# Eight neighbouring rows per partition for the experts' gate and up weights, and every eighth feature as the gather's stationary tile

## The reference

```python
def expert(y, p):
    wg, wu, wd, ge = p
    a = jax.nn.silu(t @ wg) * (t @ wu) * ge[:, None].astype(t.dtype)
    return y + a @ wd, None
```

## Time and profile before

| | |
|---|---|
| Median of 3 runs | 1677.74 us (1676.63 to 1678.19) |
| Profiled execution, own time | 1684.68 us |
| Its span | 1682.9 us |
| Mean granted TensorE clock | 0.922 |
| TensorE busy with matmuls / weight loads | 1461.1 us (87%) / 790.2 us (47%) |
| VectorE, ScalarE, GpSimd busy | 430.0, 258.2, 70.5 us |
| Moved by DMA | 345.99 MB, 206 GB/s over the span |
| Expert stage of layer 0 (gate and up of the first expert to the last down) | 410.9 to 693.5 us |
| Expert stage of layer 1 | 1301.4 to 1631.8 us |

### The profile page before, as it was taken

The page is one execution under the profiler, slowest core; times in us unless marked ns, Lnnn a source line. Parts: engine busy times, 40 slices in busy tenths (PEclk is TensorE's granted clock), DMA queues, the critical chain, the costliest instruction groups (busy, mean ns, idle before and its releaser), DMA issues.

```text
span 1682.9 us, 16791 instructions
## 1 busy us (share of the span) xinstructions
PE 1461.1 (87%) x6506; PEld 790.2 (47%) x6506; DVE 430.0 (26%) x1135; ACT 258.2 (15%) x539; POOL 70.5 (4%) x88
## 2 busy tenths in 40 slices
PE   6997997787998998479999999995995998889974
PEld 3645554444444445244454544542554443446543
DVE  3234524424111111141240613405005111111114
ACT  3033123111100000021111202111002110100001
POOL 2110100000000000100000000000000000000000
PEclk9997998897999898789999999997997999988986
DMA  9888148350999995642232333332230899994412
GB/s 336 298 281 299 57 152 319 141 191 15 395 397 396 396 396 211 228 154 100 100 100 102 105 108 110 104 104 94 79 113 9 334 396 398 395 357 162 163 34 95
DMA packets 162739, 345.99 MB, mean 206 GB/s; under 512 B 5193, under 2 KB 22642, under 8 KB 162626
## 3 DMA queue, kind: packets, MB, share of 16 engines
q1 hardware_dynamic: 149474, 318.61, 51.5%
q10 hardware_dynamic: 10208, 16.13, 2.7%
q0 software_dynamic: 2944, 9.65, 2.0%
HBM read 325.10 MB, written 19.27 MB: 205 GB/s over the span
## 4 chain that ended last, share of the span: by engine, by line
PE 78%; DMA 7%; issue 5%; DVE 5%; ACT 3%; SPq 1%; POOL 0%; ACTq 0%; DVEq 0%; POOLq 0%
PE psum L610 17%; PE psum L804 11%; PE psum L603 10%; PE psum L746 6%; DMA ring<-in_moe_w_up 6%; PE psum L822 5%; PE psum L911 5%; PE psum L768 3%; PE psum L701 3%; PE psum L901 2%; PE psum L775 2%; PE psum L573 2%; DMA ring<-in_da_w_qkv 1%; PE psum L594 1%; PE psum L713 1%
## 5 line engine op out<-in xcount | busy, mean ns | idle before, releaser
L610 PE MATMUL psum<-ring,hT 128*128 128x512 f32 x672 | 289.4, 592 | 0.0
L804 PE MATMUL psum<-ring,work 128*64 128x512 f32 x512 | 228.6, 600 | 16.0 <-DMA ring<-in_moe_w_up 9.1
L805 PE MATMUL psum<-ring,work 128*64 128x512 f32 x512 | 228.9, 600 | 0.0
L610 PEld LDWEIGHTS psum<-ring,hT 128*128 128x128 f32 x672 | 127.5, 190 | 158.9 <-issue 157.8
L603 PE MATMUL psum<-hT,ring 128*128 128x384 f32 x512 | 172.5, 497 | 10.4 <-DVE hT L1215 8.8
L746 PE MATMUL psum<-work 128*128 128x128 f32 x864 | 128.3, 305 | 23.9 <-issue 18.7
L804 PEld LDWEIGHTS psum<-ring,work 128*64 128x64 f32 x512 | 70.0, 138 | 161.5 <-issue 161.3
L746 PEld LDWEIGHTS psum<-work 128*128 128x128 f32 x864 | 114.9, 212 | 49.7 <-issue 47.4
L603 PEld LDWEIGHTS psum<-hT,ring 128*128 128x128 f32 x512 | 99.3, 194 | 79.5 <-issue 14.5
L822 PE MATMUL psum<-ring,work 128*64 128x512 f32 x256 | 117.6, 602 | 0.9 <-issue 0.9
L823 PE MATMUL psum<-ring,work 128*64 128x512 f32 x256 | 117.7, 603 | 0.0
(11 more groups left out here) (263 smaller groups left out, 1454.8 us busy)
## 6 DMA issues: line engine op xcount, KB each, us to landing
ring<-in_moe_w_gate SPq DMA_DIRECT2D x32, 2048.0 KB, 17.0
ring<-in_moe_w_up SPq DMA_DIRECT2D x32, 2048.0 KB, 21.9
ring<-in_moe_w_down SPq DMA_DIRECT2D x32, 2048.0 KB, 18.3
ring<-in_w_ada SPq DMA_DIRECT2D x24, 2048.0 KB, 11.6
ring<-in_da_w_qkv SPq DMA_DIRECT2D x6, 2048.0 KB, 17.5
expert_rows<-work ACTq DMA_DIRECT2D x64, 128.0 KB, 5.6
ring<-in_ret_w_qkv SPq DMA_DIRECT2D x8, 1024.0 KB, 8.0
ring<-in_ret_w_qkv SPq DMA_DIRECT2D x4, 2048.0 KB, 7.9
```

Source lines behind the costliest of these rows:

```text
L610: last = mm(b, hT[:, kt, P * t:P * t + P], w[:, kt, :], start=kt == 0, stop=kt == KT - 1)
L804: mm(psum[0:BLK, x, :], xk, wg[:, kt, :], start=kt == 0, stop=kt == KT - 1)
L805: last = mm(psum[BLK:P, x, :], xk, wu[:, kt, :], start=kt == 0, stop=kt == KT - 1)
```

## The change

The gate and up loads put rows `8 p` to `8 p + 7` in partition `p`, so that piece `k` of partition `p` is row `8 p + k`, and what a partition gets is 16 KB in one run of HBM. To match, the gathers take as stationary tile `kt` the features `kt`, `kt + 8`, `kt + 16` and so on of `htok`, 128 columns that stand eight elements apart. The down weights, the products and everything else stay as they were.

```diff
                 def expert_load(x, part, e):
 
                     n = (u0 + 3 * x + part) % NSLOT
-                    w = (wg, wu, wd)[part][e].rearrange("(k p) n -> p k n", p=P)
+                    w = (wg, wu, wd)[part][e]
+                    w = w.rearrange("(k p) n -> p k n", p=P) if part == 2 else w.rearrange("(p k) n -> p k n", p=P)
                     to = ring[:, n, :].rearrange("p (k n) -> p k n", k=4 if part == 2 else KT)
                     sp.dma_start(to, w).then_inc(slot_full[n], 16)
...
                         for t in range(TT):
-                            last = mm(out, htok[:, t, P * kt:P * kt + P], sel[:, t].rearrange("p x s -> p (x s)"),
+                            last = mm(out, htok[:, t, kt:D:KT], sel[:, t].rearrange("p x s -> p (x s)"),
                                       start=t == 0, stop=t == TT - 1)
...
                                 for t in range(TT):
-                                    last = mm(ov[:, OVB * kt:OVB * kt + OVB], htok[:, t, P * kt:P * kt + P], osel[:, t, :],
+                                    last = mm(ov[:, OVB * kt:OVB * kt + OVB], htok[:, t, kt:D:KT], osel[:, t, :],
                                               start=t == 0, stop=t == TT - 1)
```

## The result

The changed kernel takes 1784.5 us (median of 4, 1781.6 to 1788.0) against 1678.0 for the one before: ratio 1.063, 95% interval 1.061 to 1.066. It is 6% slower where 1660 us was forecast; what happened is the dear weight load, the rival at 1768 us, and it cost more than its price. The profiled execution took 1785.1 us, with a span of 1783.3.

What follows compares the result with a forecast made beforehand. TensorE bounds most of the kernel, DMA the two expert stages, losing 2.5 us per expert. 1684.7 - 19.5 (loads) + 2.1 (shared DMA) + 0 (strided tile) = 1667.3, less 7.0 from profiled execution to median: 1660 us; range 1655 to 1778.

Steps and rivals of the forecast that it cites:

- the dear weight load: Rival: the strided weight load at gathers L746 and L768 costs double, +110 us, 1768 us in all; chance 0.34.
- part 3: Strided stationary tile at gathers L746 and L768, 1,200 weight loads: taken to cost 0 us.
- Which end?: Choice for the gathers' weight loads between no cost and a doubled read; took 0 us, by VectorE's L1185.
- The size of the dear end: Gathers' weight loads, upper end: a doubled read adds about 100 ns to each of 1,200, some 110 us.
- Part 1: Gate and up loads at L511: 0.49 us less per load, waits before L804 go, 19.5 us less.
- The piece price: Loads at L511: a 16 KB piece takes 616 ns, 426 GB/s; a load 4.93 us instead of 5.42.
- the vanished waits: Eight waits ahead of the gate and up product L804, 15.9 us, all go at 0.49 us less per load.
- the two products at the lower clock: Gate and up products after two waits, 8.8 us against 7.0 at full clock: 3.6 us go with the waits.
- Part 2: Stalls inside the gathers, read as late instructions, grow 0.27 us each behind 16 KB pieces: +2.1 us.
- That nothing covers the gather: First gather of an expert, between gate product and transposes: no idle time would hide added weight-load time, about 100 ns each.
- unchanged pieces: Rival at the L511 loads: pieces stay 2 KB or the rate is at its ceiling, 1678 us; chance 0.12.
- 985 ns per piece: Rival at the L511 loads: a 16 KB piece takes 985 ns, a load 7.9 us, 1735 us in all; chance 0.04.

Runs made afterwards that it cites:

- rows8_packed: Changed kernel's 16 KB loads kept, gathers of the kernel before, `htok` written permuted so the stationary tile is contiguous; 1659.2 us, 0.986 of the kernel before.

## Why the prediction was wrong

- **The step that failed** is in part 3, "Which end?": of two ends, 0 and a doubled read, I took 0, by the row of a VectorE reduction from PSUM. That row was read rightly (distance cost it nothing) and was the wrong kind of row. Reads of PSUM by VectorE and ScalarE do not pay for distance. SBUF does, for reads by TensorE and for writes by VectorE and ScalarE, and here this cost 129.8 us of TensorE's time (96.0 + 33.8) where the sum had 0. The text said "another engine and memory" and weighed it as evidence nevertheless. The prediction had no row of a long f32 access to SBUF at a distance, so both ends had to keep about equal weight, and what it quoted of the Trainium skill against the change was the only statement on that memory.
- **The size of the dear end** was too small: 110 us for 129.8 measured. A read twice as long, 104 ns more, was assumed; 128 lines take about 240 ns, 2.3 times the 104. That the lower clock gives a discount was right, since a piece of 18 takes 4.62 us there against the 4.18 before, but the discount was larger than put down: 1,200 times the 126 ns of the full clock would be 151 us, 21 more than measured, where the prediction took off 10. With 130 for 110 the rival gives 1677.7 + 130 - 19.5 = 1788, near the 1784.5. At 110 it ended at 1768, and a tenth more was all the room that the range had above it.
- **Part 1 was right.** The piece price (616 ns forecast; a 16 KB packet takes 611 at the median, and the stream moves 431 GB/s), the packet count, the vanished waits and the 3.6 us of the two products at the lower clock are all there. With the gathers of before, `rows8_packed`, it is worth 0.986, somewhat more than the 0.990 that parts 1 and 2 forecast. It could not show in the change, since the gathers made TensorE slower than the loads.
- **Part 2 was not borne out**: the idle time of the gathers is 24.6 us for 23.9 with the larger pieces, +0.7 where +2.1 was put down. Whether the stalls are instructions that come late, no run shows.
- **That nothing covers the gather** held: 24 matmuls, each longer by 126 ns, are 3.02 us, and the expert's period grew by 3.03 us.
- The rivals of unchanged pieces and of 985 ns per piece did not occur.

## What to carry to other kernels

A layout that suits the DMA must not be paid for at the operand that an engine reads again and again: if columns of an f32 operand in SBUF come to stand more than 8 bytes apart (here, per weight load, 12 cost half as much as 32, and 16 nearly as much), put the permutation into a copy that is made once, and there on the side of PSUM. Of two bounds of an unknown cost, a row of another memory does not choose; a small kernel that has only the suspected access would. Larger pieces help a stage that is bound by DMA only up to where the engine beside it takes over, and the waits accumulated, divided by the number of loads before them, tell beforehand how much per load is enough.

## What the runs showed of the hardware that was not expected

- TensorE's weight loads behave as if each 16-byte line of SBUF took 1.8 ns, at either granted clock: 128 f32 columns need 233 to 238 ns at distances of four and eight elements, and 175 at three. The moving operand costs about as much at four (18 matmuls in 4.26 us against 4.40).
- VectorE's and ScalarE's writes to SBUF pay alike (692 to 1097 ns and 597 to 1122 for 128 x 512 f32); their reads from PSUM 32 bytes apart pay nothing (692 and 597).
- DMA pieces of 16 KB run at 431 GB/s on one core, over the 412 of the best stretch of 4 KB pieces, as a fixed cost of some 9 ns per piece would have it. The stalls inside the gathers, which the prediction took for late instructions, grow by no more than 0.7 us beside them. What those stalls are was not tried.
